# The weight queue waits for the issue of the first gather, not for its landing, in a streaming MLA, GLA and MoE layer

## The reference

```
h2 = rmsnorm(x, g_norm_ffn)
g_prob = softmax(h2 @ w_rg + b_rg);  p_top, g_top = top_k(g_prob, 1)
e_logits = (h2 @ w_re + b_re).reshape(n, 4, 8);  v_top, i_top = top_k(e_logits[g_top], 2)
gates = softmax(v_top) * p_top
y = sum over the two experts e of gates * ((silu(xb @ w_gate[e]) * (xb @ w_up[e])) @ w_down[e])
x = x + y;  out = rmsnorm(x, g_norm_final)
```

## Time and profile before

| | |
|---|---|
| median of 3 runs | 1079.92 us (1079.51 to 1081.91) |
| the profiled execution | 1079.81 us |
| its span, first to last instruction | 1078.0 us |
| PE matmul busy | 981.7 us (91%) |
| DVE, ACT, POOL busy | 390.0, 284.3, 209.9 us |
| DMA | 267.56 MB, mean 248 GB/s |
| granted TensorE clock, mean | 0.963 |

### The profile page before, as it was taken

One profiled execution on the slowest core, in us unless ns is written; L12 is line 12 of the kernel. 1 busy time (PEld: TensorE's weight loads), 2 busy tenths in 40 slices (PEclk: granted clock), 3 DMA queues, 4 the chain that ended last, 5 costly groups with the idle time before them and its releaser, 6 DMA issues.

```text
span 1078.0 us, 15248 instructions
## 1 busy us (share of the span) xinstructions
PE 981.7 (91%) x6278; PEld 686.4 (64%) x6278; DVE 390.0 (36%) x760; ACT 284.3 (26%) x490; POOL 209.9 (19%) x121
## 2 busy tenths in 40 slices
PE   8999999999999999999999999789778777978885
PEld 5987788889989999999996333333333333333332
DVE  7155944434787433312425121111110111111118
ACT  5435435544576621222204000000000000000012
POOL 0321222223311353443310011110110111011000
PEclk9999999999999999999998999999998889988898
DMA  9442432122121323433658999999999999999994
GB/s 220 98 92 78 126 100 60 40 79 70 50 60 31 108 79 99 148 93 99 258 242 311 416 428 424 425 426 427 427 427 429 427 427 427 427 428 425 426 413 162
DMA packets 108943, 267.56 MB, mean 248 GB/s; under 512 B 21821, under 2 KB 88797, under 8 KB 95666
## 3 DMA queue, kind: packets, MB, share of 16 engines
q1 hardware_dynamic: 104178, 258.06, 62.5%
q0 software_dynamic: 4704, 8.64, 2.1%
HBM read 256.12 MB, written 18.17 MB: 254 GB/s over the span
## 4 chain that ended last, share of the span: by engine, by line
PE 61%; DMA 26%; DVE 6%; issue 3%; ACT 3%; POOL 1%; SPq 0%; DVEq 0%; ACTq 0%; POOLq 0%
PE proj L1086 33%; DMA we<-in_w_exp_up 21%; PE proj L1554 11%; DMA we<-in_w_exp_down 4%; PE proj L1570 4%; PE bank L1231 2%; PE bank L1258 1%; PE bank L1244 1%; PE bank L1450 1%; DVE xsT L2623 1%; PE bank L1580 1%; ACT ex L1910 1%; PE proj L1556 0%; DVE hT_f L2147 0%; DMA x_rows<-in_x_prompt 0%
## 5 line engine op out<-in xcount | busy, mean ns | idle before, releaser
L1554 PE MATMUL proj<-we,xsT 128*64 128x512 f32 x512 | 250.1, 646 | 66.6 <-DMA we<-in_w_exp_up 59.4
L1556 PE MATMUL proj<-we,xsT 128*64 128x512 f32 x512 | 250.6, 647 | 0.0
L949 POOL TENSOR_TENSOR wlo<-raw,whi 128x1024 fp32r<-128x1024 f32 x68 | 156.5, 2302 | 383.7 <-PE proj L1086 359.6
L1554 PEld LDWEIGHTS proj<-we,xsT 128*64 128x64 f32 x512 | 73.2, 149 | 209.1 <-issue 193.5
L1086 PE MATMUL proj<-hT_hi,whi 128*128 128x272 f32 x688 | 147.0, 295 | 2.5 <-POOL wlo L949 1.4
L1086 PE MATMUL proj<-hT_hi,wlo 128*128 128x272 f32 x688 | 145.2, 292 | 0.0
L1086 PE MATMUL proj<-hT_lo,whi 128*128 128x272 f32 x688 | 145.0, 292 | 0.0
L2615 DVE TENSOR_TENSOR hg<-hg,proj 64x512 f32<-64x512 f32 x32 | 22.1, 690 | 307.0 <-ACT hg L2066 293.6
L2066 ACT ACTIVATE hg<-proj 64x512 f32<-64x512 f32 x30 | 17.7, 590 | 421.9 <-PE proj L1556 421.9
L1570 PE MATMUL proj<-we,hT 128*64 128x512 f32 x256 | 115.2, 592 | 2.0 <-DVE hT L2618 1.1
L1571 PE MATMUL proj<-we,hT 128*64 128x512 f32 x256 | 115.2, 593 | 0.0
(11 more groups left out here) (391 smaller groups left out, 1391.7 us busy)
## 6 DMA issues: line engine op xcount, KB each, us to landing
we<-in_w_exp_gate SPq DMA_DIRECT2D x31, 2048.0 KB, 32.2
we<-in_w_exp_up SPq DMA_DIRECT2D x31, 2048.0 KB, 36.7
we<-in_w_exp_down SPq DMA_DIRECT2D x31, 2048.0 KB, 39.0
raw<-in_w_in SPq DMA_DIRECT2D x43, 512.0 KB, 3.9
x_rows<-in_x_prompt SPq DMA_DIRECT2D x8, 512.0 KB, 5.0
raw<-in_w_branch_b SPq DMA_DIRECT2D x8, 512.0 KB, 4.1
raw<-in_w_out SPq DMA_DIRECT2D x8, 512.0 KB, 4.1
zc<-expert_out SPq DMA_DIRECT2D x4, 1024.0 KB, 17.3
```

What stands on the lines that cost most here:

```text
L949: nc.gpsimd.tensor_tensor(lo[:, 0:c], raw[n % NRAW][:, 0:c], hi[:, 0:c].bitcast(F32), ALU.subtract).then_inc(w_split, 1)
L1554: pe.matmul(proj[0:SLOTS, s, 0, :], xsT[:, k, cols], wg[:, k * FF:(k + 1) * FF], start=(k == 0), stop=(k == KD - 1))
L1556: mm = pe.matmul(proj[64:64 + SLOTS, s, 0, :], xsT[:, k, cols], wu[:, k * FF:(k + 1) * FF], start=(k == 0), stop=(k == KD - 1))
```

## The change

SP's wait ahead of the last two parts of expert 2 is for `dispatched` ≥ 1 instead of `xs_loaded` ≥ 16, and POOL's first increment of `dispatched` stands right behind the first gather instead of right ahead of the second.

```diff
@@ -871,7 +871,7 @@
         sp.wait_ge(x2_turned, 7 + NT)
         load_expert(1, 2, 1)
 
-        sp.wait_ge(xs_loaded, 16)
+        sp.wait_ge(dispatched, 1)
         load_expert(2, 1, 2)
         load_expert(2, 2, 2)
 
@@ -984,10 +984,10 @@
         pool.wait_ge(rows_stored, 16 * NT)
         pool.wait_ge(gidx_ready, 1)
         gather(xsb, P, xs_loaded)
+        pool.sem_inc(dispatched, 1)
         pool.wait_ge(ys_zeroed, 16 * NZERO)
 
         pool.wait_ge(gidx_ready, 2)
-        pool.sem_inc(dispatched, 1)
         gather(xsb, P, xs_loaded)
```

## The result

The changed kernel takes 1088.62 us (median of 4 runs, 1087.94 to 1089.11), the kernel before, measured beside it, 1079.72 us (4 runs, 1079.32 to 1081.91). The ratio is 1.0076, with a 95% interval of 1.0063 to 1.0088 (it is not the ratio of the two medians). By medians the kernel is 8.9 us slower, outside the range of the prediction. The span of the profiled execution is 1086.1 us against 1078.0.

A forecast was written before the change was run, and what follows sets the result against it. The late weight stream and its last hole were taken to bound the kernel. Gather 2.5, less 0.2 slack, plus clock 1.5, less credit 1.7 gave +2.1 us on 1079.92: 1082.0 us, range 1078.2 to 1085.8.

The forecast's parts named there:

- What bounds the kernel: Second half is one stream of expert weights at 427 GB/s; its end depends on where the last hole lies.
- First part: SP, released by POOL's increment at about 581.7, issues expert 2's up and down parts 3.2 us sooner.
- A sign that I had named for being wrong: The prediction is wrong if, in the changed profile, the first up product starts later than 592.
- Second part: Moving POOL's increment from ahead of the second gather to behind the first costs 0.
- Fourth part: First gather shares the DMA engines with expert 2's weights and lands 2.5 us later; less 0.2, PE is 2.3 late.
- rival B: Increment goes out at the gather's hand-over, weights queue first: gather pays 4.8 us, end +4.4 to some +6; chance 0.20.
- The clock: PE idles twice around the first transposes, its clock falls to 0.50, costing 1.5 us of product.
- Third part: Expert 3's up part lands 12.4 us after issue into an empty queue, so the end moves by D - 1.7 us.
- D: What the change delays PE's first up product and so expert 3's loads: 2.3 + 1.5 = 3.8 us.
- slack: PE's idle 0.44 us ahead of the first transposes, partly busy with matmuls, covers 0.2 us of the gather's delay.
- Rivals C, D and E: C: gather not delayed, 1078.2, chance 0.14; D: gather late, clock holds, 1080.5, 0.16; E: change does nothing, 1079.9, 0.04.

The follow-up runs named there:

- the memset: Changed kernel with a small POOL memset behind the first gather instead of the bare increment, SP waiting for its completion: 1079.1 us, ratio 1.0005.
- gate_rows_done: Kernel before, with SP waiting for the stored rows and PE's gate_rows_done instead of the gather's landing: 1079.37 us, ratio 0.9999.
- 5 fillers: Kernel before, with 5 filler matmuls on PE between the transposes and the first up product, release as before: 1082.77 us, ratio 1.0028.
- meta_ready: Kernel before, with SP waiting for the stored rows and DVE's meta_ready instead of the gather's landing: 1079.83 us, ratio 1.0002.
- the increment alone: Changed kernel with SP waiting for the gather's landing as before, POOL's increment left behind the first gather: 1080.22 us, ratio 1.0002.
- 11 fillers: Kernel before, with 11 filler matmuls on PE between the transposes and the first up product, release as before: 1087.45 us, ratio 1.0081.

## Why the prediction was wrong, point by point

**What bounds the kernel** held: one stream of weights to the end, at 427 GB/s in both kernels, and the last hole decides. That PE and SP both hang on the gather, and that the hole would only move to expert 3's issue, held too. One reading was off, without consequence: in the 40 slices the DMA engines are at 9 tenths from the twenty-third on, from some 593 us, and not from slice 19.

**First part, the moment of the release**: failed, and it is the step that decided. I wrote that the increment behind the gather's instruction "runs at about 581.7", after the 1.18 us of its row. SP issued 0.19 us before the row started. The increment released SP ahead of the work. A sign that I had named for being wrong followed: the first up product started at 593.75, later than 592; expert 3's loads went out at 602.33 and not at 598.6. The Trainium skill has the rule that I should have weighed (GPSIMD Engine Reference, section Instruction dispatch): an instruction's completion holds back whoever waits on its own semaphore, and not the next instruction on Pool. The traces show more than that sentence says: the bare increment took effect before the gather's row had even begun, while the memset in the same place started at 580.57, when that row ended.

**Second part, the increment's place costs nothing**: held, 1.0002.

**Fourth part, the price of the contention**: mis-sized for both orders. 2.5 us was set on a gather with weights just behind it. That case is the kernel with the memset, and costs nearly nothing. The case that came about, weights just ahead, cost 7.4 us (11.9 against 4.5), at the upper bound from the third gather, 12.1, and beyond the 4.8 that rival B took from the second. I had called the second gather the nearest row. The nearest by state was any gather that finds the weight queue filled and stays behind it from its first packet to its last; that is the steady state, in which the median of the sixteen gathers of the trace is 12.2 us.

**The clock**: taken at 1.5 us for two idle stretches of 2.3 and 1.4. The idle was 7.06 us, and it cost 0.92 + 1.45 = 2.4. Right in kind; the idle was longer than I had it, and the fall already covers the transposes.

**Third part, the credit of 1.7 us**: failed. Expert 3's up part was to land 12.4 us behind its issue; it took 13.2, and a second slow stretch of 1.1 us followed that the rule did not have. The lead of 1.9 us in bytes was gone 20 us later, 181.98 MB being left in both kernels. In the table the end is 483.0 to 484.0 us behind expert 3's issue in ten profiles out of eleven, with expert 2 in flight at that moment or long landed; the eleventh has 486.3. The end moves by D, or a little more.

The sum with the measured terms: 7.4 for the gather, 0.2 of slack, 2.4 for the clock, and 0.6 by which the end lies further behind expert 3's issue (483.8 against 483.2, no more than profiles differ in that): 7.4 - 0.2 + 2.4 + 0.6 = 10.2 us from the start of the gather, where I had 2.5 - 0.2 + 1.5 - 1.7 = 2.1. **Rival B** named what happened, weights ahead of the gather because the increment goes out at the hand-over, and I gave it 0.20. Its price of +4.4 to +6 fell short by its 4.8 for the gather, by the same 1.7 of credit, and in its first figure by 0.9 of clock. Rivals C, D and E are out: the gather was late, the clock fell, and SP was released.

## What to carry to other kernels

Before a release is costed by the end of an instruction's row, ask which event really sends it: the completion of work, or a bare increment that the queue reaches first. A small transfer that others wait for must be in the DMA queues before a large one is let go; one microsecond of order (a release 0.68 or 1.54 us behind the gather's start) was worth 6.6 us at the first up product here, and behind a filled queue its price was near that of the gathers in the steady state, not that of the nearest in time. And a stream is not free again when its hole is over: count the restart. Having the next loads queued before the last have landed brought 2.6 us at best here.

## What the runs showed of the hardware that I had not expected

- A bare semaphore increment that stands behind an indirect DMA on POOL let SP issue 0.19 us before that DMA's row began (two profiles of two).
- A gather of 0.27 MB ahead of 4 MB of weights lands in 4.3 to 4.5 us, as if alone; behind them it takes 10.7 to 11.9. Its first packet then comes 3 to 5 us after the start of its row instead of some 2. The Trainium skill's rule that each DMA engine takes its queues in turn, a packet at a time (DMA: Bandwidth & Descriptors, section Queues, rings and completion order), fits the mixed packets, 144 and 209 in the changed kernel; it doesn't tell of the late first packet.
- After a restart of the empty weight queue there are two slow stretches, in the first 2 us and 10 to 13 us later, worth 0.8 and 1.1 us in the changed kernel. Against a queue that still had 0.79 MB of the loads before, all of that lead was lost within 20 us.
- The granted clock fell to 0.50 for some 3 us after idle stretches of only 0.79 and 1.38 us with 1.16 us of transposes between them. How little an idle stretch settles is seen at the next one: behind the same 1.5 us between the first two up products the clock stayed at 1.00 in the kernels before, with gate_rows_done and with 5 fillers, and fell to 0.50 for some 3 us in those with meta_ready, with the memset, with the increment alone and with 11 fillers.
